# Sample attention: the products for the maxima spread two to a step over all sixteen steps, two steps ahead of the tile border

## The reference, cut to what matters

```python
def grid_attention(q, k, v, q_gain, k_gain):
    ...
    def one_block(qi):
        s = jnp.einsum('bkgqd,bskd->bkgqs', qi, kh).astype(jnp.float32)
        p = jax.nn.softmax(s, axis=-1).astype(vh.dtype)
        return jnp.einsum('bkgqs,bskd->bqkgd', p, vh)

    o = lax.map(one_block, qb)
```

## Time and profile before

| | |
|---|---|
| median of three runs | 3398.29 us (3397.72 to 3399.98) |
| span of the profiled execution | 3395.9 us |
| TensorE busy, whole span | 2941.8 us, 87% |
| VectorE busy, whole span | 2312.9 us, 68% |
| ScalarE busy, whole span | 1558.7 us, 46% |
| 800 to 1550 us: TensorE, VectorE, ScalarE busy | 714.46, 569.65, 274.48 of 750 us |

### The profile page before, as it was taken

One profiled execution on the slowest core, in us unless ns is written; L12 is line 12 of the kernel. 1 busy time (PEld: TensorE's weight loads), 2 busy tenths in 40 slices (PEclk: granted clock), 3 DMA queues, 4 the chain that ended last, 5 costly groups with the idle time before them and its releaser, 6 DMA issues. The chain is left out here.

```text
span 3395.9 us, 42658 instructions
## 1 busy us (share of the span) xinstructions
PE 2941.8 (87%) x13075; PEld 2019.0 (59%) x13075; DVE 2312.9 (68%) x2874; ACT 1558.7 (46%) x1980; POOL 592.2 (17%) x395
## 2 busy tenths in 40 slices
PE   6999999579999999996996599958999999999940
PEld 3776776434444444443664378747877778787730
DVE  2665565337777777774776544458888888888856
ACT  2323333003333333335553233217777777787744
POOL 0000000000000000002893000012323333332335
PEclk8999999669999999998997689969999999999975
DMA  6112111550111111100003433347577876678347
GB/s 250 50 47 70 51 41 59 174 142 19 38 31 24 37 33 23 37 13 7 1 0 130 142 122 125 120 154 272 209 276 274 305 292 241 230 271 317 146 173 309
DMA packets 237754, 446.17 MB, mean 131 GB/s; under 512 B 21377, under 2 KB 95197, under 8 KB 236925
## 3 DMA queue, kind: packets, MB, share of 16 engines
q1 hardware_dynamic: 222277, 397.67, 34.5%
q0 software_dynamic: 15408, 47.73, 3.7%
q10 hardware_dynamic: 8, 0.01, 0.0%
HBM read 367.45 MB, written 86.29 MB: 134 GB/s over the span
## 5 line engine op out<-in xcount | busy, mean ns | idle before, releaser
L2177 DVE TENSOR_TENSOR weights_rest<-w,weights_rounded 128x2048 fp32r<-128x2048 f32 x315 | 716.1, 2287 | 114.5 <-ACT weights_rounded L2110 113.4
L2110 ACT ACTIVATE weights_rounded<-w 128x2048 fp32r x315 | 602.7, 1922 | 144.1 <-PE ps_up L2032 74.0
L833 ACT ACTIVATE probs<-ps_scores 128x1024 f32<-128x1024 f32 x260 | 266.0, 1023 | 503.5 <-PE ps_scores L764 415.6
L856 DVE TENSOR_REDUCE part_max<-ps_max 128x1 f32<-128x512 f32 (+1 forms) x528 | 338.0, 677 | 193.6 <-PE ps_max L741 193.5
L425 PE MATMUL ps_proj<-w_in,n1T 128*128 128x512 f32 (+2 forms) x1152 | 346.6, 459 | 6.5 <-PEq L108 6.5
L2032 PE MATMUL ps_up<-weights_rounded,block_T_rounded 128*128 128x512 f32 x832 | 334.8, 402 | 5.8 <-DVE block_T_rest L2185 5.8
L2032 PE MATMUL ps_up<-weights_rounded,block_T_rest 128*128 128x512 f32 x832 | 325.8, 392 | 0.0
L2032 PE MATMUL ps_up<-weights_rest,block_T_rounded 128*128 128x512 f32 x832 | 324.5, 390 | 0.0
L774 PE MATMUL ps_attn<-probs,v 128*64 128x512 f32 x1040 | 283.6, 625 | 0.0
L425 PEld LDWEIGHTS ps_proj<-w_in,n1T 128*128 128x128 f32 x1152 | 196.6, 191 | 144.8 <-issue 130.3
L741 PE MATMUL ps_max<-kT,q_for_max 128*128 128x512 f32 (+1 forms) x528 | 191.2, 435 | 76.1 <-DVE part_max L856 41.5
(11 more groups left out here) (353 smaller groups left out, 4913.4 us busy)
## 6 DMA issues: line engine op xcount, KB each, us to landing
w<-in_w SPq DMA_DIRECT2D x96, 2048.0 KB, 11.9
expert_rows<-scratch_y SPq DMA_DIRECT2D x36, 512.0 KB, 8.9
w_ada_rest<-in_w_ada SPq DMA_DIRECT2D x5, 2048.0 KB, 15.6
scratch_qT<-qT_stage SPq DMA_DIRECT2D x18, 512.0 KB, 3.5
q_for_max<-scratch_qT SPq DMA_DIRECT2D x36, 256.0 KB, 5.7
q_rounded_twice<-scratch_qT SPq DMA_DIRECT2D x36, 256.0 KB, 4.4
mix_rows<-scratch_mix SPq DMA_DIRECT2D x18, 512.0 KB, 5.1
scratch_h<-h_rows SPq DMA_DIRECT2D x18, 512.0 KB, 2.6
```

What stands on the lines that cost most here:

```text
L833: act.activation(pf[:, slot(p, n), :], ps_s[:, n % 2, :], ACT.Exp).then_inc(exp_done, 1)
L856: nc.vector.tensor_reduce(mx[:, p, n // H, n % H:n % H + 1], ps_m[:, n % 2, 0:PART], AX.X, ALU.max).then_inc(m_taken, 1)
L2110: act.activation(split_piece(wh, s), raw_piece(s, buf[0]), ACT.Copy).then_inc(hi_done, 1)
L2177: nc.vector.tensor_tensor(split_piece(wl, s), raw_piece(s, buf), split_piece(wh, s).bitcast(F32), ALU.subtract).then_inc(lo_done, 1)
```

## The change

For the sample, `M_STEPS` becomes 16 and a new `M_AHEAD` = 2 shifts the products by two steps: steps 0 to 13 of tile t issue the pairs 2 to 15 for tile t + 1, and steps 14 and 15 issue pairs 0 and 1 for tile t + 2. `maxima_in` says which products stand in a step, for TensorE and VectorE alike. The first four products for tile 1 come ahead of the loop, behind the row of tile 0. In step 14 the row now stands directly behind the scores, then the weighing, then the two products. For the prompt the order stays what it was.

```diff
-    M_STEPS = max(1, NS - 2)
+    M_STEPS = NS if g else 1
+    M_AHEAD = 2 if g else 0
...
+        def maxima_in(t, p, step):
+
+            c = step + M_AHEAD
+            ahead, chunk = (1, c) if c < NS else (2, c - NS)
+            if chunk >= M_STEPS or (isinstance(t, int) and t + ahead >= NQ):
+                return
+            for m in range(chunk * NM // M_STEPS, (chunk + 1) * NM // M_STEPS):
+                yield t + ahead, (p + ahead) % 2, m
...
             row(0, 0)
+            for m in range(M_AHEAD * NM // M_STEPS):
+                maximum(1, 1, m)
...
                     score(t, p, n)
-                    if not is_last(t):
-                        for m in range(n * NM // M_STEPS, min(NM, (n + 1) * NM // M_STEPS)):
-                            maximum(t + 1, 1 - p, m)
-                    follow(t, p, n)
-                    if n == ROW_STEP and not is_last(t):
+                    if n == ROW_STEP and g:
+                        if not is_last(t):
+                            row(t + 1, 1 - p)
+                        follow(t, p, n)
+                    for at in maxima_in(t, p, n):
+                        maximum(*at)
+                    if n != ROW_STEP or not g:
+                        follow(t, p, n)
+                    if n == ROW_STEP and not g and not is_last(t):
                         row(t + 1, 1 - p)
```

## The result

The changed kernel takes 3354.19 us, the median of four runs (3353.9 to 3355.17), against 3398.01 us for the kernel before in the same comparison: a ratio of 0.9871, with a 95% interval of 0.9857 to 0.9885. The forecast was 3350.5 within 3343 to 3366. The profiled execution's span fell by 43.7 us, from 3395.9 to 3352.2.

The account below looks back on a forecast made before the run. TensorE, 95% busy, was taken to bound the sample attention. Tiles 0 to 13 save 45.2 us, tile 14 4.4, the prologue costs 2.0: 47.6 us off, forecast 3350.5 us, range 3343 to 3366.

Parts of the forecast that it names:

- The third products are the gain: Steps 3, 6, 10 and 13: removing third products saves 4.44 us a tile, 3.50 after 0.94 comes back.
- The row finds `neg_max` ready: Step 14: `neg_max` done at 904.87, row can start at 905.35; 0.48 us to spare, so no cost.
- The chain row, copy, product: Step 14: first product waits for ScalarE's copy of the row; weighing hides all but 0.27 us; step takes 4.71 us.
- Step 15 becomes a plain step: Step 15, last of the tile: with its pair it takes 2.61 us instead of 2.14.
- The sum: Whole stage: 45.2 us from tiles 0 to 13, 4.4 from tile 14, less 2.0 for the prologue, 47.6 us.
- VectorE's lateness is absorbed in steps 0 to 2: Behind the tile border: VectorE about 1.0 us late; step 2 loses 0 to 0.6 us, taken as 0.
- Rival 1: Behind the border: VectorE's lateness returns as one wait a tile, 1.32 us, 18 us over 14 tiles, 3369; chance 0.10.
- The prologue costs 2.0 us: Before the first score: four products for tile 1 run at VectorE's pace, adding 2.0 us; range 1.0 to 6.
- The fear for the clock: Prologue: pauses between the four products may drop TensorE's clock, first steps up to 1.87 times as long; range 6 us.
- The gain reaches the end: After the stage: what follows starts behind a barrier with operands loaded, so the whole gain should reach the end.
- rival 2: Step 14: waiting for the copy drops TensorE's clock; 51 us slower, about 3447; chance 0.06, any other loss included.

Follow-up runs that it names:

- adding first: Changed kernel with VectorE in step 14 doing its addition ahead of the two reductions instead of behind them; median 3351.15 us, stage 720.09 us.
- three and one after folds: Changed kernel with products spread unevenly: three in steps 1, 4, 6 and 9, one in steps 2, 5, 7 and 10; 3430.18 us.
- one pair ahead: Changed kernel rearranged with `M_AHEAD` 1: no pair in step 14, one in step 15, two in step 11, two products in the prologue; 3343.41 us.
- weighing ahead of the row: Changed kernel with the weighing put back ahead of the row of maxima in step 14, the two products directly behind the row; 3369.64 us.
- both pairs in step 15: Changed kernel with step 14's pair moved into step 15, the weighing between the two pairs, VectorE adding before it reduces; 3350.92 us.
- three and one in calm steps: Changed kernel with products spread unevenly: three in steps 3, 6, 10 and 12, one in steps 4, 7, 11 and 13; 3404.76 us.

## Why the prediction was right, point by point

- *The third products are the gain.* Right, and shown: taking the evenness away alone gives all of it back (49.6 us), at 0.82 us for each third product where the steps of before had given 0.81 (1.04 less the 0.23 of an even one).
- *The row finds `neg_max` ready.* Right: done at 898.47, row at 898.98.
- *The chain row, copy, product.* Right as a mechanism, 0.2 us short: forecast 4.71 for step 14 from score to score, measured 4.90. The passing on from the copy took 0.24 us instead of 0.15, and the next score came 0.56 us behind the product (902.17 to 902.73) where 0.47 was added. At the borders of tiles 0 and 1, which stand outside the loop, the passing on took 0.10 us; why is not shown. Doubling the copy and undoing the order both showed that it stands on the path.
- *Step 15 becomes a plain step.* Wrong by size, and the term that was missed: forecast 2.61, measured 2.76. The prediction put no wait there. Its own numbers show how close it was: they place the step's second product at 908.93 + 1.04 + 0.23 = 910.20 and have its bank reduced at 908.46 + 0.42 + 1.29 = 910.17, without the passing on. As these numbers have it, the pair came 1.50 us after that of step 14 (902.17 to 903.67, 1.51 by them). But the reductions began 0.53 us after their product instead of 0.42: a pair that follows a wait takes 0.72 us here, a plain one 0.63 (912.71 in the earlier trace rows). So the bank was late, and the weighing behind lost 0.25 us; 0.1 us came back, as the pair follows its score by 0.94 us (902.73 to 903.67) instead of 1.04.
- *The sum.* Steps 14 and 15 together take 7.66 us instead of 4.71 + 2.61 = 7.32: 0.25 for the bank and 0.09 for the passing on (the late score of step 14 and the early pair of step 15 cancel). The fourteen tiles saved 42.0 us instead of 45.2, which is all that the stage lacks: the forecast was 47.6 us, the stage gave 44.5, the span 43.7. (By its own terms, 3398.29 - 47.6, the forecast is 3350.7, not 3350.5.)
- *VectorE's lateness is absorbed in steps 0 to 2.* Right: they take 2.61 us each. I had kept up to 0.6 us for step 2. Rival 1 held the mechanism that did come, a wait for VectorE's reductions once a tile, but in step 15 and at 0.25 us, not 1.32; and it is not lateness, since VectorE sits idle before those reductions and adding first changed nothing.
- *The prologue costs 2.0 us.* Right: 2.07. The fear for the clock was idle in this execution, not in others (below).
- *The gain reaches the end.* Right: 43.7 of the stage's 44.5 us are in the span, and this stage began 1.0 us later.
- *The clock falls at the border* (rival 2). Not so in the changed kernel: 1.00 over 670 us. That it can fall inside the stage, behind a wait of TensorE, is shown all the same by three and one after folds (last section).

## What to carry to other kernels

Where an engine fills two banks that another empties, count the time between one fill and the next, not the sum of the work: here a pair of products cost 0.47 us and no wait when it came 1.57 us behind the pair before and both banks were back in time (step 11 of one pair ahead), 0.25 us more when it came 1.50 us behind one whose reductions had begun late, and a third product straight behind a pair cost 1.04 us in all, even with VectorE on time. Spread evenly first, without any change of what waits for what (62% of the gain here), and look ahead only for the steps that this cannot fill. Where a copy has to come between, put work that doesn't need it behind its start, and move the consumer to the far side of that work rather than right behind the copy.

## What the runs showed of the hardware

The clock can fall again right after it rose. In the changed kernel's profile it stayed up; in that of the variant that adds first, which issues the same instructions on TensorE, it was granted 0.71 and then 0.50 of full speed (1.2 GHz) just behind the four products of the prologue, while TensorE was at work nearly all the time:

```profile
756.00:762.00 6.00, 4.30 (x19) 2.18 (x17) 1.01 (x2) 1.01 (x1) 0.00 (x0) 0.72 0.81 126
762.00:764.00 2.00, 1.90 (x6) 1.38 (x6) 1.56 (x3) 0.00 (x0) 0.00 (x0) 0.71 0.00 0
764.00:766.00 2.00, 2.00 (x7) 1.54 (x6) 1.09 (x2) 1.03 (x1) 0.00 (x0) 0.50 0.00 0
768.00:772.00 4.00, 4.00 (x17) 1.64 (x15) 3.45 (x6) 2.01 (x2) 0.00 (x0) 1.00 0.00 0
```

There the first exponential came 8.72 us after the row began instead of 8.04, the first two stood 2.26 us apart instead of 1.41, and tile 0 took 44.51 us instead of 43.65: 1.5 us lost in all. The bound kept for it, up to 4 us, was not reached. The products before had waited 0.55 us for VectorE between their pairs, after 1.15 us in which TensorE stood idle. The profiles of the weighing ahead of the row and of three and one after folds show the same fall. Six of the profiles have the same order on TensorE up to there: three fell and three (changed, both pairs in step 15, three and one in calm steps) did not.

In the steady tiles (812 to 1480 us), nine of the ten profiles kept a granted clock of 1.00, with single waits of up to 1.3 us on TensorE. In the tenth, three and one after folds, the clock fell in tiles 4, 8, 10 and 11, each time right behind the third product of step 1, which had waited 1.39 to 1.50 us; such a tile took 54.0 to 54.1 us instead of 52.5. In tile 4 (the wait, then a stretch of 2 us with a mean granted clock of 0.62):

```profile
977.82 0.49 PE L752 MATMUL ps_max<-kT,q_for_max 128*128 128x512 f32 x1 [1.49 <-DVE part_max L873]
```

```profile
978.00:980.00 2.00, 2.00 (x6) 0.24 (x6) 1.05 (x2) 0.00 (x0) 0.00 (x0) 0.62 0.32 51
```

In the ten other tiles from 1 to 14, waits of 1.39 to 1.49 us at the same place left it up. What decides it stays open, here as at the start: the same program did both, and nothing was tried that tells the cases apart.
